# State tables around the token tiles, u read back by two queues, and the first block projected for all tokens first

## What is computed

```
h    = rmsnorm(x) * (1 + sc1) + sh1           # sc1, sh1 from silu(cond) @ w_ada
proj = h @ w_in                               # 1024 -> 1024
pool_out = pool_mixer(proj[:, :512])
ssm_out  = ssm_mixer(proj[:, 512:])           # u; 32 groups of 16 channels, 64 complex states
x = x + g1 * concat(pool_out, ssm_out) @ w_out
x = x + g2 * square(relu(h2 @ w_mlp1)) @ w_mlp2
```

## Time and profile before

| | us |
|---|---|
| three runs | 1267.06, 1269.73, 1270.05 |
| median | 1269.73 |
| profiled execution: its own time | 1267.13 |
| profiled execution: span on the core | 1265.3 |
| busy: PE, DVE | 1177.7, 850.8 |
| busy: ACT, POOL | 333.6, 440.8 |

### The profile page before, as it was taken

How to read it: one execution, slowest core, us unless ns; L and a number is a source line. 1 busy time by engine, 2 the same in 40 slices (tenths; PEclk the granted TensorE clock), 3 DMA queues, 4 the chain that set the end, 5 groups by cost and what they waited for, 6 DMA issues and landing times.

```text
span 1265.3 us, 18409 instructions
## 1 busy us (share of the span) xinstructions
PE 1177.7 (93%) x6417; PEld 1027.3 (81%) x6417; DVE 850.8 (67%) x1347; ACT 333.6 (26%) x621; POOL 440.8 (35%) x370
## 2 busy tenths in 40 slices
PE   6799997735899999999999999999999999999997
PEld 0389995424787888989989989899899899898896
DVE  5889999999795677456465564564564654645648
ACT  4554324323334673101102112011011021120114
POOL 1000001401000533372562652743724626527430
PEclk9889998677899999999999999999999999999999
DMA  9606425963412232011021120120110210201003
GB/s 326 208 20 138 113 101 191 255 174 103 163 36 84 83 117 67 18 50 50 17 66 33 33 66 33 33 66 17 50 50 16 66 38 28 66 33 33 33 1 150
DMA packets 63347, 101.99 MB, mean 81 GB/s; under 512 B 9518, under 2 KB 45422, under 8 KB 63052
## 3 DMA queue, kind: packets, MB, share of 16 engines
q1 hardware_dynamic: 56616, 79.97, 20.6%
q0 software_dynamic: 5168, 17.93, 4.5%
q10 hardware_dynamic: 1524, 3.56, 0.9%
HBM read 89.86 MB, written 9.49 MB: 79 GB/s over the span
## 4 chain that ended last, share of the span: by engine, by line
PE 69%; DVE 25%; issue 2%; ACT 2%; DMA 1%; ACTq 1%; DVEq 0%
PE bank L1372 22%; PE bank L1374 22%; PE bank L1373 22%; DVE fold_p L1070 2%; DVE fold_q L1068 2%; DVE fold_q L1069 2%; PE bank L1381 2%; DMA raw<-in_w_ada 1%; DVE sums L1171 1%; DVE x_lo L981 1%; DVE states_a L1076 1%; DVE states_a L1073 1%; DVE states_b L1073 1%; DVE states_b L1076 1%; DVE acc L1356 1%
## 5 line engine op out<-in xcount | busy, mean ns | idle before, releaser
L507 POOL TENSOR_TENSOR acc<-acc,gated 128x512 f32<-128x512 f32 x270 | 372.6, 1380 | 376.2 <-DVE gated L1308 339.6
L1372 PE MATMUL bank<-x_hi,w_hi 128*128 128x384 f32 x960 | 324.0, 337 | 4.1 <-issue 2.7
L1374 PE MATMUL bank<-x_hi,w_lo 128*128 128x384 f32 x960 | 321.6, 335 | 0.0
L1373 PE MATMUL bank<-x_lo,w_hi 128*128 128x384 f32 x960 | 321.5, 335 | 0.0
L1308 DVE TENSOR_TENSOR gated<-bank,gate_b 128x512 f32<-128x512 f32 x270 | 183.1, 689 | 115.0 <-PE bank L1374 102.0
L1372 PE MATMUL bank<-w_hi,f_hi 128*128 128x512 f32 x576 | 224.2, 389 | 1.2 <-DVE w_lo L1289 1.2
L1374 PE MATMUL bank<-w_hi,f_lo 128*128 128x512 f32 x576 | 224.4, 390 | 0.0
L1373 PE MATMUL bank<-w_lo,f_hi 128*128 128x512 f32 x576 | 224.3, 389 | 0.0
L852 ACT ACTIVATE relu<-bank 128x384 f32<-128x384 f32 x96 | 47.2, 493 | 649.4 <-PE bank L1374 646.4
L1298 DVE TENSOR_TENSOR f_tmp<-relu 128x384 f32<-128x384 f32 x96 | 64.3, 670 | 206.0 <-ACT relu L852 206.0
L1372 PEld LDWEIGHTS bank<-x_hi,w_hi 128*128 128x128 f32 x960 | 180.7, 188 | 7.8 <-issue 6.1
(11 more groups left out here) (294 smaller groups left out, 1320.8 us busy)
## 6 DMA issues: line engine op xcount, KB each, us to landing
raw<-in_w_mlp SPq DMA_DIRECT2D x64, 512.0 KB
raw<-in_w_ada SPq DMA_DIRECT2D x48, 512.0 KB
out<-acc SPq DMA_DIRECT2D x9, 512.0 KB, 2.6
x_tile<-in_x_sample POOLq DMA_DIRECT2D x8, 512.0 KB, 8.9
raw<-in_w_in SPq DMA_DIRECT2D x8, 512.0 KB
raw<-in_w_out SPq DMA_DIRECT2D x8, 512.0 KB
x_again<-in_x_sample POOLq DMA_DIRECT2D x8, 512.0 KB, 3.6
u_rows<-proj ACTq DMA_DIRECT2D x4, 576.0 KB, 2.8
```

What stands on the lines that cost most here:

```text
L507: GP.tensor_tensor(a, a, BT[i % 4][:], ALU.add).then_inc(s.acc, 1)
L1372: mm(out, sh_, mh, start=first, stop=False)
L1373: mm(out, sh_, ml, start=False, stop=False)
L1374: return mm(out, sl, mh, start=False, stop=last)
```

## The change

- **Tables around the tiles (DVE).** The eight `to_state` calls are put elsewhere and into the order TABLES: 0 and 1 where the power chain stood, 2 behind the normed tiles, 3 and a part of 4 in the tile loop, the rest of 4, then 5 and 6 behind it, and 7 within scan(0) after its second fold, with split_lo(3). The temporary is TPQ for the first three and a new buffer TPB for the others. To make room, the x tiles, the dump of the squares and TPB move: x tiles 0 to 5 now lie where the weight splits and the b tables will, so ScalarE's split 1 waits for four turned tiles.
- **Power chain on POOL.** Its 32 operations are issued by POOL after the x tiles, and DVE waits for them ahead of scan(0).
- **First block for all tokens first.** IN_SEQ starts with block 0 for groups 0, 1, 2, then block 1 for 0, 1, 2; before, it alternated blocks 0 and 1 by group. BESIDE loses its entry at tile 7, and tile 8 has the whole of projection 1.
- **Turned tables.** Half tables of block a are turned behind projections 2, 3 and 4, those of block b behind 23 (before: 9 to 12), over three banks. States of block a come behind projections 4 and 7 (before: 7 and 8).
- **u by two queues.** SP reads back the even tokens of a chunk and POOL the odd ones, four DMAs each per block; SP loads the last two w_in blocks behind them.
- **SPLIT_AT** is (2, 8, 14, 19) instead of (1, 8, 14, 19).

The core of the diff:

```diff
+STATES_AT = (4, 7)
-SPLIT_AT = (1, 8, 14, 19)
+SPLIT_AT = (2, 8, 14, 19)
-WB_AT = {3: (0, 1), 4: (2, 3), 5: (4, 5), 6: (6, 7), 9: (8, 9), 10: (10, 11), 11: (12, 13), 12: (14, 15)}
-IN_SEQ = [(i, g) for g in range(NG) for i in range(2)] + [(i, g) for i in range(2, 8) for g in range(NG)]
+WB_AT = {2: (0, 1, 4, 5), 3: (2, 3), 4: (6, 7), 23: tuple(range(8, 16))}
+WB_ORDER = [k for a in sorted(WB_AT) for k in WB_AT[a]]
+TABLES = [(0, 0, 0), (0, 0, 1), (0, 1, 0), (0, 1, 1), (1, 1, 0), (1, 1, 1), (1, 0, 0), (1, 0, 1)]
+IN_SEQ = [(i, g) for i in range(2) for g in range(NG)] + [(i, g) for i in range(2, 8) for g in range(NG)]
-BESIDE = {4: (0, 0, 3), 5: (0, 3, 6), 6: (0, 6, 8), 7: (1, 0, 3), 8: (1, 3, 8)}
+BESIDE = {4: (0, 0, 3), 5: (0, 3, 6), 6: (0, 6, 8), 8: (1, 0, 8)}
...
# SP
-            for j in range(L):
-                sp.dma_start(U[b][j * SP:(j + 1) * SP, 8 * h:8 * h + 8, :], ud[:, :, j * CH:(j + 1) * CH]).then_inc(u_in[b][h], 16)
+            for j in range(0, L, 2):
+                sp.dma_start(u_dst(b, h, j), u_src(b, h, j)).then_inc(u_in[b][h], 16)
-        for i in range(N_IN - 1):
+        for i in range(N_IN - 2):
             load_in(i)
         for h in range(2):
             load_u(0, h)
-        load_in(N_IN - 1)
+        for i in range(N_IN - 2, N_IN):
+            load_in(i)
...
# POOL, behind the x tiles
+            gp.wait_ge(s.powers, 1)
+            next_(GP.tensor_scalar(AQ[0:N, :], PI[0:N, L, :], 1.0, None, ALU.mult))
+            next_(GP.tensor_scalar(AQ[N:P, :], PI[N:P, L, :], -1.0, None, ALU.mult))
...
+            for i in range(6):
...
+                next_(GP.tensor_tensor(dr, sr, sr, ALU.mult))
+                next_(GP.tensor_tensor(di, si, si, ALU.mult))
+                next_(GP.tensor_tensor(dr, dr, di, ALU.subtract))
+                next_(GP.tensor_tensor(di, sr, si, ALU.mult))
+                next_(GP.tensor_scalar(di, di, 2.0, None, ALU.mult))
...
+        for h in range(2):
+            load_u(0, h)
...
# ACT, split_hi
+                elif w == 1:
+                    act.wait_ge(s.tr, 4)
...
# DVE
-        power_chain()
+        to_state(0, TPQ)
+        to_state(1, TPQ)
         for t in range(TT):
             normed(t, XS[t][:], XS[t][:], 0)
+        to_state(2, TPQ)
...
+            if t == 0:
+                to_state(3, TPB, (0,))
+            if t == 4:
+                to_state(4, TPB, (0,))
             round_lo(t, HT0, 0)
...
+            if t == 3:
+                to_state(3, TPB, (1, 2))
...
-        to_state(0, 0, 0, 1)
-        to_state(0, 0, 1, 2)
-        to_state(0, 1, 0, 3)
-        to_state(0, 1, 1, 4)
+        to_state(4, TPB, (1, 2))
+        to_state(5, TPB)
+        to_state(6, TPB)
         split_lo(2, FIRST_IN + 2)
-        to_state(1, 0, 0, 5)
-        split_lo(3, FIRST_IN + 3)
-        to_state(1, 0, 1, 6)
-        to_state(1, 1, 0, 0)
-        to_state(1, 1, 1, 7)
         def beside_first(k):
+            if k == 1:
+                to_state(7, TPB)
+                split_lo(3, FIRST_IN + 3)
...
+        dve.wait_ge(s.chain, 32)
         scan(0, beside_first)
...
# PE, states
-                pe.wait_ge(u_in[b][i // 8 % 2], 16 * L)
+                pe.wait_ge(u_in[b][i // 8 % 2], 16 * L // 2)
+                pe.wait_ge(u_gp[b][i // 8 % 2], 16 * L // 2)
...
-            if a in (7, 8):
-                for p_ in range(8 * (a - 7), 8 * (a - 6)):
+            if a in STATES_AT:
+                for p_ in range(8 * STATES_AT.index(a), 8 * STATES_AT.index(a) + 8):
                     states(p_)
```

More of the change, by code:

```diff
@@ L66, in build @@
     RAW = [at(f"raw{i}", [P, 1024], R_RAW + i * 4 * KBYTE) for i in range(4)]
-    XS = [at(f"x_tile{i}", [P, D], R_W + (16 + 4 * i) * KBYTE if i < 2 else R_A + 4 * (i - 1) * KBYTE) for i in range(TT)]
-    SQ0 = at("square_dump0", [P, D], R_A)
+    XS = [at(f"x_tile{i}", [P, D], R_W + 4 * i * KBYTE if i < 6 else R_A + 4 * (i - 1) * KBYTE) for i in range(TT)]
+    SQ0 = at("square_dump0", [P, D], R_A + 16 * KBYTE)
+    TPB = at("table_tmp", [P, D], R_A + 16 * KBYTE)
     HT0 = [at(f"h_tile{i}", [P, KB, P], o) for i, o in enumerate((R_S, R_P, R_P + 10 * KBYTE))]
@@ L186, in build @@
     u_in = [[s.u_in0, s.u_in1], [s.u_in2, s.u_in3]]
+    u_gp = [[s.u_gp0, s.u_gp1], [s.u_gp2, s.u_gp3]]
     loc_in = [s.loc_in0, s.loc_in1]
@@ L272, in in_order, with u_dst, u_src, wb_bank @@
         return ap.rearrange("p (k r j) -> p k r j", r=NR, j=L)
+    def u_dst(b, h, j):
+        return U[b][j * SP:(j + 1) * SP, 8 * h:8 * h + 8, :]
+    def u_src(b, h, j):
+        i = 2 * b + h
+        return UD[i * P:(i + 1) * P, j * CH:(j + 1) * CH].rearrange("(g p) t -> p g t", p=SP)
+    def wb_bank(k):
+        n = WB_ORDER.index(k)
+        return BANK[4 + n % 4] if n < 8 else BANK[5 + (n - 8) % 3]
     @block.sync
@@ L424, in _, with power_chain, next_, load_u @@
                 gp.dma_start(XS[t][:], x_prompt[:]).then_inc(x_in[t], 16)
+        def power_chain():
+            done = [0]
+            def next_(ins):
+                done[0] += 1
+                ins.then_inc(s.chain, 1)
+                gp.wait_ge(s.chain, done[0])
+            gp.wait_ge(s.powers, 1)
+            next_(GP.tensor_scalar(AQ[0:N, :], PI[0:N, L, :], 1.0, None, ALU.mult))
+            next_(GP.tensor_scalar(AQ[N:P, :], PI[N:P, L, :], -1.0, None, ALU.mult))
+            sr, si = (v.rearrange("p (d b g) -> p d b g", d=2, b=2) for v in (PR[:, L, :], AQ[:]))
+            for i in range(6):
+                dr, di = AR_[i][:], AI_[i][:]
+                if i == 0:
+                    dr, di = (v.rearrange("p (b d g) -> p d b g", d=2, b=2) for v in (dr, di))
+                next_(GP.tensor_tensor(dr, sr, sr, ALU.mult))
[3 more added lines that the diff above has]
+                next_(GP.tensor_scalar(di, di, 2.0, None, ALU.mult))
+                sr, si = AR_[i][:], AI_[i][:]
+        power_chain()
+        def load_u(b, h):
+            gp.wait_ge(uds[2 * b + h], 16)
+            for j in range(1, L, 2):
+                gp.dma_start(u_dst(b, h, j), u_src(b, h, j)).then_inc(u_gp[b][h], 16)
+        for h in range(2):
+            load_u(0, h)
         def skip_weights():
@@ L434, in _ @@
             gp.dma_start(dst[N:P], second[:]).then_inc(s.cs_in, 16)
+        for h in range(2):
+            load_u(1, h)
         gp.wait_ge(s.in_mm, 24)
@@ L933, in _, with to_state @@
         then(tt(ZI[:], M3[:], RD[:], ALU.mult))
-        def to_state(b, d, h, ready):
+        def to_state(n, tmp, ops=(0, 1, 2)):
+            b, d, h = TABLES[n]
             gs = slice(b * GB + 8 * h, b * GB + 8 * h + 8)
@@ L941, in to_state @@
             b1, b2 = (t_[:, q0:q0 + 8, :].unsqueeze(2).to_broadcast([P, 8, L, SP]) for t_ in (B1, BY))
-            tmp = TPQ[:, 0:8 * P].rearrange("n (g j p) -> n g j p", g=8, p=SP)
-            tt(tmp, b2, pi, ALU.mult).then_inc(s.dve, 1)
-            tt(out, b1, pr, ALU.mult).then_inc(s.dve, 1)
-            count[0] += 2
-            dve.wait_ge(s.dve, count[0])
-            tt(out, out, tmp, ALU.add).then_inc(s.wbt if ready else s.wbt_first, 1)
-            dve.wait_ge(s.wbt if ready else s.wbt_first, max(ready, 1))
+            tmp = tmp[:, 0:8 * P].rearrange("n (g j p) -> n g j p", g=8, p=SP)
+            if 0 in ops:
+                tt(tmp, b2, pi, ALU.mult).then_inc(s.dve, 1)
+                count[0] += 1
+            if 1 in ops:
+                tt(out, b1, pr, ALU.mult).then_inc(s.dve, 1)
+                count[0] += 1
+            if 2 in ops:
+                dve.wait_ge(s.dve, count[0])
+                tt(out, out, tmp, ALU.add).then_inc(s.wbt, 1)
+                dve.wait_ge(s.wbt, n + 1)
         def from_state(b, d, h):
@@ L1008, in _ @@
             then(tt(PR[:, hi, :], PR[:, hi, :], PT[0][:, 0:n, :], ALU.subtract))
-            then(tt(PI[:, hi, :], PI[:, hi, :], PT[1][:, 0:n, :], ALU.add))
+            ins = tt(PI[:, hi, :], PI[:, hi, :], PT[1][:, 0:n, :], ALU.add)
+            if n < 4:
+                then(ins)
+            else:
+                ins.then_inc(s.powers, 1)
+                dve.wait_ge(s.powers, 1)
         dve.wait_ge(s.b_in, 64)
@@ L1445, in turn_wb @@
                 pe.wait_ge(s.aff_d, 4 * TT)
[L1446 to L1449 removed]
+            if 4 <= n < 8:
+                pe.wait_ge(s.wb_ready, n - 3)
+            elif 8 <= n < 11:
+                pe.wait_ge(s.st_act, 16)
+            elif n >= 11:
+                pe.wait_ge(s.wb_ready, n - 2)
             for q in range(4):
[L1451 removed]
+                last = PE.transpose(wb_bank(k)[:, q * P:(q + 1) * P], WB[b][:, d, 4 * i + q, :], ID[:])
             last.then_inc(s.wbt_mm, 1)
```

40 lines of the change are left out of this document (9 added, 31 removed).

## The result

| | before | after |
|---|---|---|
| median, us (runs taken side by side) | 1267.81 | 1274.18 |
| profiled execution: time, span | 1267.13, 1265.3 | 1276.48, 1274.7 |
| busy: PE, DVE | 1177.7, 850.8 | 1180.4, 844.2 |
| busy: ACT, POOL | 333.6, 440.8 | 334.4, 474.7 |
| from_state starts | 194.33 | 202.54 |

The changed kernel is slower: 1274.18 us (1272.62 to 1276.48) against 1267.81 (1266.79 to 1270.05), ratio 1.0048, 95% interval 1.0037 to 1.0058, so 6.1 us by the ratio (6.4 between the medians), with 1275 predicted. PE does the same work as before, and DVE's is less by the power chain that POOL took over (850.8 to 844.2, POOL 440.8 to 474.7); what grew is time in which both wait. The profiled execution of after is its longest: its from_state is 8.2 us late and its span 9.4 longer.

The account below looks back on a forecast made before the run. DVE's scan and PE's projections were taken to bound the front, meeting at from_state; 0.4 + 3.5 + 2.9 = +6.8 us gave 1273.9 for a profiled-like execution, 1275 with half the median's offset; range 1268.5 to 1281.

Parts of the forecast that it names:

- What bounds the kernel: Front of the kernel: DVE's scan(0) and PE's in_mm 24 meet at from_state, whose shift passes whole to the end.
- Part 1, +0.4: DVE ahead of the first affine: tables replace the power chain, ada columns reached at 52.95, first rounded tile 0.4 us later.
- Part 2, +3.5: Power chain on POOL beside full DVE: handovers lose 0.2 or 0.12 us each, 3.5 us in all, bounds 0 and 6.
- The first rival: POOL's short operations slip in for nothing; total +3.3, 1270.4 to 1271.7 us; chance 22%.
- Part 3: Tiles to scan: scan starts at 103.7 instead of 115.48, but u of block 1 lands at 118.5 (bounds 117.5, 120.5).
- The rival of a late half on POOL: POOL's half of the u reads comes late, its issues held by DVE; +2 to 3 us, 1278; chance 8%.
- PE's clock: Rival: PE's clock falls in the new idles; one projection at half speed is +4.2 us, 1279; chance 10%.
- Part 4, +2.9: Split behind the third fold: DVE waits for w_hi, fourth fold starts at 130.4 instead of 127.45; +2.9 us, bounds +1.9, +5.
- The signs named: Expected in the profile: POOL operations with waits, slower DVE tables, later first affine and fold, PE and DVE waits, from_state about 201.
- the two signs of being wrong: DVE's normed tiles ending before 51, or DVE going from the third fold to the split without a wait.
- Behind from_state: After from_state the shift was to pass on whole to the end, the tail being PE's and untouched.

Follow-up runs that it names:

- experiment 5: Changed kernel with the power chain's 32 operations back on DVE, right ahead of scan(0), POOL having none: 1274.67 us, ratio 1.0044.
- Experiments 6: Changed kernel with a memset and eight extra POOL additions of 128x512 floats on a spare buffer ahead of the power chain: 1279.95 us, ratio 1.0098.
- 7: Changed kernel with a memset and eight extra POOL additions of 128x256 floats on a spare buffer ahead of the power chain: 1275.46 us, ratio 1.0058.
- experiments 2: Changed kernel, but SP issues the last two w_in loads only when all of u's block 1 has landed: 1271.54 us, ratio 1.0027.
- 8: Changed kernel with all eight reads of a block of u issued by SP, none by POOL, w_in behind them: 1271.16 us, ratio 1.0022.
- experiment 1: Changed kernel with SPLIT_AT = (5, 8, 14, 19) instead of (2, 8, 14, 19), a later split of weight block 4: 1271.22 us, ratio 1.0018.
- experiments 4: Changed kernel with STATES_AT = (5, 7) instead of (4, 7) and SPLIT_AT = (5, 8, 14, 19): 1267.23 us, ratio 0.9988 to the kernel before.
- 9: Changed kernel with all reads of u issued by SP and the split of weight block 4 behind the fifth fold: 1268.12 us, ratio 1.0001.
- 11: Changed kernel with old projection order, states of block a behind projections 6 and 7, SPLIT_AT (5, 8, 14, 19), two queues: 1263.05 us, ratio 0.996.

## Why the prediction was right, and where it wasn't

The time was right within 1 us, its sign too, and that is in good part luck. The sum had one term too large (POOL's chain, 3.5 us that were not there) and one too small (the delay at the fourth fold, 8.2 instead of 2.9), and these cancelled but for 1.4 us. A second pair cancelled as well: an execution like the profiled one was put at 1273.9 and took 1276.48, but the median, put 1.3 above that, came 2.3 below it.

- **What bounds the kernel: right.** from_state was the moment to look at; DVE's delay there of 8.21 us is found again at 323 us (x_lo 323.13 before, 331.34 after), and PE's idle ahead of the y blocks (26.8 before, 28.4 after) took up the moved half tables.
- **Part 1, +0.4: about right.** Without contention the columns were to be reached at 52.95. They were at 52.75, but with 0.5 of contention in them: the first table began at 33.43 where the chain had begun at 34.14. The first affine was 0.2 later than before, and the first rounding not at all. The three table pieces among the tiles cost nothing: the ninth h_lo came at 84.1 as before.
- **Part 2, +3.5: wrong in its price.** The step that failed is "a straight line gives 0.25, and 0.2 of that is lost at each end". The picture was right: 32 small operations from 29.3 to 56.5, most with a wait for DVE inside them.

```profile
33.63 1.21 POOL L461 TENSOR_TENSOR a_re<-a_re,a_im_signed 128x64 f32<-128x64 f32 x1
...
52.94 0.29 POOL L460 TENSOR_TENSOR a_im_signed<-a_im_signed 128x64 f32<-128x64 f32 x1
```

DVE, the same table operation with POOL beside it (after) and without (experiment 5):

```profile
50.12 1.34 DVE L1002 TENSOR_TENSOR to_state_a<-b_bar,pow_re 128x1024 f32<-128x1024 f32 x1
```

```profile
49.89 1.22 DVE L1000 TENSOR_TENSOR to_state_a<-b_bar,pow_re 128x1024 f32<-128x1024 f32 x1
```

An operation of the chain lasts 1.21 beside two-input operations of DVE and 0.29 when DVE's operation leaves it alone. But DVE lost next to nothing: two tables took 7.54 us (33.43 to 40.97) where six operations of before give 7.32, the normed tiles 7.88 instead of 7.83, the third table 3.90 instead of 3.66, 0.5 in all. Nearly all of it is in four of the nine table operations, 0.10 to 0.12 each; the other five lost nothing. Experiments 6 and 7 show that a small operation was not to be charged by its length: some 0.4 to 0.55 of POOL's operation is hidden at each handover, so one of 0.3 costs little or nothing. Experiment 5 shows that it costs no time in the whole. The first rival had this step right. Why part of a handover is hidden stays open. (The Trainium skill, "SBUF — State Buffer", "SBUF: two separate sides", has an exclusive lock for the whole instruction, on which the prediction leaned. The long operations here agree in kind, each side waits for the other; at 0.73 for one that lasts 1.28, the measured price is below the whole instruction.)
- **Part 3: the gain right, u wrong.** States(0) were to start at 100.9 and did at 101.20, the scan at 103.7 and did at 104.03, u's store at 110.0 and was at 110.32. The term that was mis-sized is u: the 3.9 us of transfer had the DMA engines to itself in the sum, and the two w_in loads that the change puts right behind it, named in the description of the change, were not charged. With them 120.81 instead of 118.5, beyond the bound of 120.5; without them 119.27 and 118.89 (experiments 2 and 8), inside the bounds. The two terms that were charged came out: the 3.9 and the 1.8 of latency, for which no row stood, are together 5.7 from the first issue to the states, and experiments 2 and 8 have 5.74 and 5.66. But 150 GB/s is not what full DMA engines move at most, as they moved 264 at the same share of 1.17, and 0.63 us for an issue of SP, the mean of sixteen in before, was too much: in experiment 8 eight issues took 3.62, not 5.0. So the issues of one queue were never slower than the transfers. The rival of a late half on POOL did not come: its four issues took 2.10 us, 0.53 each, from 113.38.
- **PE's clock.** It was kept as a rival with 10% and priced for a projection behind the idle ahead of a=2, where it did not fall. It fell at the states of block 1, in the idle that the late u made, and cost 2.9 us there. Third fold: 125.53 instead of 121.2.
- **Part 4, +2.9: mechanism right, size wrong.** The wait on w_hi behind the third fold is there, 5.30 instead of 4.3. It was mis-sized by what stands ahead: states(8) 2.3 later and 2.9 longer give the fourth fold 5.2 more than forecast (135.62 against 130.4), while part 2 gave none of its 3.5. At from_state +8.2 where +6.8 was the sum. The same lateness holds for PE: in_mm 24 at 198.2 where 193.4 was forecast, still ahead of DVE.
- **The signs named.** Seen: 32 small operations on POOL with waits inside, PE waiting for u, DVE waiting ahead of the third fold (9.47, forecast 6) and for w_hi (5.30, forecast 4), from_state at 202.54 (201). Not seen: table operations of 1.4 (1.23 to 1.34), a first affine at 57 to 58 (54.21), a first fold 3.9 us behind 103.7 (104.03). And one of the two signs of being wrong came true: the normed tiles ended before 51, at 48.85. It is the sign of part 2.
- **Behind from_state** the prediction had the shift passed on as it is. In the profiled execution 1.1 us more is lost, in the clock of PE after 331 us. The stretches of before and of after, each from just behind the same x_lo (323.13 and 331.34):

```profile
325.00:327.00 2.00, 2.00 (x8) 2.00 (x7) 2.00 (x3) 1.98 (x3) 0.58 (x2) 0.50 0.03 8
327.00:329.00 2.00, 2.00 (x11) 2.00 (x10) 1.42 (x2) 1.24 (x2) 0.53 (x1) 0.83 0.58 209
```

```profile
333.00:335.00 2.00, 2.00 (x8) 2.00 (x7) 2.00 (x3) 1.98 (x3) 0.37 (x1) 0.50 0.06 14
335.00:337.00 2.00, 2.00 (x7) 2.00 (x7) 1.31 (x2) 1.34 (x2) 0.74 (x2) 0.50 0.59 168
```

PE's granted clock rises about two us later behind that x_lo (at 327.7 before, at 338.3 after), and two us more at half speed are the 1.1. What decides that isn't settled; nothing in the change touches this stage.

**The spread.** The states of block 1 took 7.04 us in the profile of after, 5.83 in experiment 1, 5.70 in experiment 5, and 4.16 in experiments 6 and 7, where PE had been idle for 2.86 and 2.19 us in the same place. So the clock falls there in some executions and not in others, and an idle's length alone did not tell which. In after and experiment 5 it fell while PE still stood idle, in experiment 1 about one us after the states had begun. That the median of after is 2.3 us below its profiled execution fits this, but the other executions have no trace, so it stays open.

## What to carry to other kernels

An earlier start is worth only what the next dependency lets through: follow the new order to the first place where it waits again (here the read back of the second block, and a split whose data now came later), and compare its time there, not at the start. A transfer on the critical path is to be charged with every load that the change lets go at the same moment, and a second queue for it may only let these go sooner. And before an order is rejected, its constants are worth a try: the new order with two constants changed was as fast as before, and the same tables in the old order, with states one projection earlier and a split three folds later, were 5 us faster.

## What the runs showed of the hardware

- A GpSimd operation beside a two-input operation of VectorE costs VectorE less than its own length: 0.73 for 128x512 floats (1.28 long), 0.30 for 128x256, 0 to 0.12 for 128x64 (0.29 long). For GpSimd itself the small operation grows from 0.29 to about 1.2 us.
- A GpSimd memset does not hold a two-input operation of VectorE (beside the memset of 1.18 us at 251.27 in before VectorE's folds took the usual 0.45 to 0.46), but a copy of 128x16 floats that met one took 1.28, 1.23 and 1.11 instead of 0.18 (experiments 4, 9 and 11).
- Eight reads of 72 KB issued by two queues landed no earlier than by one (states at 119.27 and 118.89, 5.74 and 5.66 us behind the first issue). With two loads of 512 KB issued right behind them it was 7.0 to 7.7 us.
- TensorE was granted 0.50 after an idle of 2.2 to 2.9 us in three executions (after, experiments 1 and 5), and its full clock after idles of 2.2 and 2.86 in two others (experiments 7 and 6).
